# Hybrid attention / RG-LRU / expert kernel on one Trainium2 core: v split by sequence, turned heads on every second step, a postponed first product, and the last expert by column halves

## The chip, the cores and the metric

The kernel runs on one core of one Trainium2 chip. The metric is device time in microseconds (us), lower is better. The engines are PE (TensorE), DVE (VectorE), ACT (ScalarE), POOL (GpSimd) and SP (SyncE, which here only issues DMAs).

## The reference, cut to what matters

One encoder layer, applied with the same weights to two sequences of 512 tokens of width 1024. All data are float32.

```python
h = rmsnorm(x, norm1_g)
q, k, v, xr, gate = split(h @ w_in)          # 8 query heads, 2 key/value heads of 64; LRU width 512
q, k = rope(rmsnorm(q)), rope(rmsnorm(k))
attn_out = softmax(q @ k.T / 8) @ v          # per head, 512 x 512, not causal
lru_out = (scan forward + scan backward of conv(xr)) * gelu(gate)
x = x + concat(attn_out, lru_out) @ w_out
h2 = rmsnorm(x, norm2_g)
# expert choice: each of 16 experts takes its 64 best tokens of each sequence
ys = (silu(xs @ w_gate[e]) * (xs @ w_up[e])) @ w_down[e] * gate_vals
out = x; out[tok_idx] += ys
```

## The kernel before, in words

**Numbers in two parts.** Every matrix product takes a float32 operand as a sum of two rounded parts, `_hi` and `_lo`. ACT writes the hi part, DVE (or POOL) subtracts it from the original for the lo part, and PE makes three matmuls: hi x hi, hi x lo, lo x hi (`product`, lines 972 to 974). Transposes run on PE too, against an identity (line 978), four blocks of 128 x 128 into one PSUM bank.

**Order by hand.** Each engine walks through the same Python list of steps and takes its own part of each; engines meet through semaphores. There is one program order per engine, so whatever stands behind a waiting instruction waits too.

**Stage 1, projections and the LRU.** 28 jobs (7 groups of 4) project the input; `LRU_AT[n]` lists what the engines do beside job n. The last group is the gate of LRU channels; its last job is n = 27. q and k of sequence 0 are rotated, normalised and split here ("rotate", "norm", "hi", "lo"); the last of the ten rotate/norm units (unit 9, k of sequence 1) is left for the attention stage.

**Stage 2, attention.** A list `attn` holds slots 0 to 73. There are 64 units u (16 heads x 4 blocks of 128 queries). In slot u

- PE makes the scores of unit u (two matmuls, lines 1107 and 1108), the four transposes of the probabilities of unit t = u - 6, and the product with v of unit v = u - 8;
- DVE takes the row maximum of unit u (line 1453), the reciprocal of the row sum of unit u - 1 (line 1462), and `probT_lo` of unit t (line 1465);
- ACT writes `probT_hi` of unit t (line 836) and the exponential of unit u (line 843);
- POOL scales the probabilities of unit u - 1 (line 619).

PE's scores of u wait for the exponential of u - 3, its transposes of t for `probT_lo` of t - 3 and, where t begins a head, for all four scaled units of that head; its product of v waits for `probT_lo` of v. Two heads form a pair and add into one bank. Pairs 0, 1 and 2 use the same bank 6, so the first product of pairs 1 and 2 (v = 8 in slot 16, v = 16 in slot 24) waits until ACT and DVE have taken the pair before out of it (`mixA_hi` line 828, `mixA_lo` line 1459), which they do in that same slot.

`beside` (line 374) adds work to single slots. "hi"/"lo" split q and k of blocks 4 to 7 (sequence 1), "v" splits all of v (ACT line 809, then DVE line 1448), "rotate"/"norm" 9 finish unit 9. Twelve "transpose" steps, n = 12 to 23, turn the heads of sequence 1 through the one bank 7 (`turn_heads`): each waits for the "out" step of the one before, in which ACT (even n, line 703) or DVE (odd n, line 1321) copies the bank. Transpose n stands in slot 10 + (n - 12) * 5 // 3 and its out in the slot after. From slot 34 on, the splits of `w_out` and of the LRU output stand there too. SP loads the first three rows of `w_out` once "lo" 7 is done.

**Stage 3** is the output projection, norm and routing. **Stage 4** is a loop over the 16 experts, 24 weight rows each; a row is split by ACT (line 899) and DVE (line 1619) into one of six slots and used by six matmuls (two column halves of 512). At the end ACT scales the expert's output into `ys` (line 914) and POOL adds it to y by an indirect accumulating DMA (`scatter_step`, line 655).

Of the kernel before, what the change touches and what calls it, by code (L numbers as in the profile page):

```python
# [29 lines left out]
P = 128  # L30
# [8 lines left out]
def layer_program(nc, x0, x1, norm1_g, w_in, q_norm_g, k_norm_g, conv_w, conv_b, lru_w_r, lru_b_r,  # L39
# [100 lines left out]
    v_hi = at("v_hi", R1 + 80 * K, [P, NB, VW], F32R)  # L140
    v_lo = at("v_lo", R1 + 90 * K, [P, NB, VW], F32R)
# [19 lines left out]
    assert VW * NB * 4 == 10 * K  # L161
# [30 lines left out]
    gate_all = at("gate_all", SM - 128, [P, E], F32)  # L192

# [150 lines left out]
    lru_at(26, *[(stage, n) for stage in ("transpose", "out") for n in range(BPS)])  # L344
    for n in range(NG * JOBS):
        g, j = ORDER[n]
        if n >= JOBS:
            steps.append(("project", n))
        first = [step for step in LRU_AT.get(n, []) if step[0] in ("scan",)]
        steps += first  # L350
        if n >= JOBS:
            steps.append(("empty", n - 1))
        for w in range(2, NG):
            if n == FIRST_OF[w] - (0, 0, 3, 3, 3, 3, 4)[w]:
                steps += [("w_hi", w), ("w_lo", w)]
        steps += [step for step in LRU_AT.pop(n, []) if step not in first]
# [96 lines left out]
    def v_in(v):  # L453
        return v[:, 1, :, :].rearrange("p b (g w) -> p b g w", g=KVH)
# [4 lines left out]
    def _(sp):  # L459
# [58 lines left out]
        sp.wait_ge(v_lo_done, 1)  # L518
# [66 lines left out]
    def _(pool):  # L585
# [18 lines left out]
        pool.wait_ge(proj_done, NG * JOBS)  # L604
        for v in (v_hi, v_lo):
            pool.memset(v[:, :, :].bitcast(F32).rearrange("p b (g d) -> p b g d", d=HD)[:, :, 0::2, :], 0.0).then_inc(v_zeroed, 1)
# [63 lines left out]
        for e in range(E - 4, E):  # L670
            scatter_step(e, 2 * (E - 4) + e - (E - 4) + 1)

    @block.scalar
    def _(act):
        def prepare(kind, n=0):
# [10 lines left out]
            elif kind == "hi":  # L686
                act.wait_ge(qk_norm_done, units_before(n))
                if n >= BPS:
                    act.wait_ge(rotated, UNITS_QK)
                    act.wait_ge(gates_done, 2 * CT)  # L690
                if n >= BPS + 2:
                    act.wait_ge(qkT_done, last_turn(n - 2) + 1)
                act.activation(q_pair[pair_set(n)][:, :, 0, :].rearrange("p (g h) d -> p g h d", g=2).bitcast(F32R), q_heads(n), ACT.Copy)
                act.activation(k_pair[pair_set(n)][:, :, 0, :, :].bitcast(F32R), k_heads(n).unsqueeze(2).to_broadcast([P, KVH, 2, HD]),
                               ACT.Copy).then_inc(qk_hi_done, 1)

# [10 lines left out]
        for step in steps:  # L707
# [84 lines left out]
            elif kind in PREPARE:  # L792
                prepare(kind, *arg)
            elif kind == "out":
                turn_act(*arg)
# [169 lines left out]
        act.wait_ge(row_used, 24 * E + 8)  # L965
        results(E - 1)

    @block.tensor
    def _(pe):
# [113 lines left out]

        for kind, n in attn:
# [5 lines left out]
            elif kind == "slot":  # L1090
# [24 lines left out]
                if 0 <= v < UNITS:  # L1115
                    head, kc = divmod(v, BPS)
                    pair, s = head // 2, head // HQ
                    if kc == 0 and head % 2 == 0 and pair:
                        pe.wait_ge(mixA_lo_done, pair if pair < PAIRS_ONE_BANK else pair - 1)
                    pe.wait_ge(v_lo_done, 1)  # L1120
                    pe.wait_ge(v_zeroed, 2)
                    pe.wait_ge(probT_lo_done, v + 1)
                    blk, cols = BPS * s + kc, pair_cols(head)
                    product(bank[:, out_bank(pair), :], v_hi[:, blk, cols], v_lo[:, blk, cols], probT_hi[:, kc, :], probT_lo[:, kc, :],
                            head % 2 == 0 and kc == 0, head % 2 == 1 and kc == BPS - 1).then_inc(pv_done, 1)
# [123 lines left out]
        rows(24 * E, 0, 4, hidT_hi, hidT_lo, {})  # L1249

    @block.vector
    def _(dve):
# [15 lines left out]
        def prepare(kind, n=0):  # L1268
# [38 lines left out]
            elif kind == "lo":  # L1307
# [5 lines left out]
                                  kp[:, :, 0, :, :], ALU.subtract).then_inc(qk_lo_done, 1)  # L1313

# [9 lines left out]
        for step in steps:  # L1324
# [104 lines left out]
            elif kind in PREPARE:  # L1429
                prepare(kind, *arg)  # L1430
            elif kind == "out":
# [9 lines left out]
        for kind, n in attn:  # L1441
# [4 lines left out]
            elif kind == "v":  # L1446
                dve.wait_ge(v_hi_done, 1)
                dve.tensor_tensor(v_of(v_lo), v_in(kv_nat), v_of(v_hi).bitcast(F32), ALU.subtract).then_inc(v_lo_done, 1)
# [164 lines left out]
        dve.tensor_copy(gate_all[:, :], bank[:, 6, 0:E]).then_inc(routed, 1)  # L1613

# [91 lines left out]
```

## Time and profile before

| | us |
|---|---|
| three runs | 1057.98, 1058.98, 1059.56 (median 1058.98) |
| the profiled execution | 1058.12 |
| its span, first to last instruction | 1056.2 |
| PE / DVE / ACT / POOL busy | 984.7 / 818.7 / 747.0 / 338.2 |
| mean granted TensorE clock | 0.979 of full speed |

The chain that ended last lies on PE for 82% of the span, on DVE for 7% and on ACT for 5%. By time the kernel has four parts: projections and LRU to about 209 us, attention to about 356, projection and routing to about 477, experts to the end. In a row of the timeline the first number is the start in us from the span's start, the second the duration; in square brackets stands how long the engine had been idle and what ended that.

### The profile page before, as it was taken

To read this page: it belongs to the slowest core of one execution; us is meant where nothing else is said; L and a number is where in the kernel's file an instruction comes from. 1 tells how busy PE (TensorE), PEld (TensorE's weight loads), DVE (VectorE), ACT (ScalarE), POOL (GpSimd) and SP (SyncE) were. 2 spreads that over 40 slices of the span, in tenths; PEclk is the share of its full clock that TensorE was granted. 3 is DMA by queue.
4 is the path that set the end of the run, shared out by engine and by line. 5 is a ranking of instruction groups with operands and counts; after the bars stand their busy time and mean duration, and the time that the engine had idled before them with its cause. 6 is when DMAs were issued, how large, how long until landed. Compare 5 with 4: busy or idle time off the path is not lost.

```text
span 1056.2 us, 15145 instructions
## 1 busy us (share of the span) xinstructions
PE 984.7 (93%) x5035; PEld 826.2 (78%) x5035; DVE 818.7 (78%) x1079; ACT 747.0 (71%) x1002; POOL 338.2 (32%) x175
## 2 busy tenths in 40 slices
PE   5999999977999999928999999999999999999994
PEld 4997998856777788827888888888888888888883
DVE  5749898787787224784989888988898889988983
ACT  6447888467797455545878877887788777877772
POOL 1000000132396111141056435643464346513320
PEclk9999999989999999968999999999999999999998
DMA  8110111000301633368999999999999999999842
GB/s 283 36 46 6 46 40 41 1 0 7 115 1 63 239 120 120 120 242 342 409 392 410 388 384 392 405 386 385 391 400 383 383 393 400 382 384 372 323 163 36
DMA packets 75265, 248.97 MB, mean 236 GB/s; under 512 B 9380, under 2 KB 16600, under 8 KB 75224
## 3 DMA queue, kind: packets, MB, share of 16 engines
q1 hardware_dynamic: 70616, 231.65, 57.1%
q0 software_dynamic: 4608, 16.78, 6.2%
q8 instruction: 25, 0.41, 0.2%
q14 instruction: 16, 0.13, 0.0%
HBM read 231.63 MB, written 16.78 MB: 235 GB/s over the span
## 4 chain that ended last, share of the span: by engine, by line
PE 82%; DVE 7%; ACT 5%; issue 3%; POOL 1%; DMA 1%; ACTq 0%; SPq 0%; POOLq 0%; DVEq 0%
PE bank L972 25%; PE bank L974 24%; PE bank L973 24%; PE bank L978 6%; DVE e_lo L1619 2%; ACT e_hi L899 2%; PE bank L1149 1%; PE bank L1107 1%; PE bank L1108 1%; PE bank L1007 1%; DMA x_nat<-in_x_prompt_dram 1%; ACT prob L843 1%; DMA xs<-h_rows,idx_all 0%; POOL prob L619 0%; DVE row_stat L1453 0%
## 5 line engine op out<-in xcount | busy, mean ns | idle before, releaser
L972 PE MATMUL bank<-e_hi,xsT_hi 128*128 128x512 f32 x512 | 202.4, 395 | 0.7 <-DVE xsT_lo L1624 0.6
L974 PE MATMUL bank<-e_hi,xsT_lo 128*128 128x512 f32 x512 | 200.5, 392 | 0.0
L973 PE MATMUL bank<-e_lo,xsT_hi 128*128 128x512 f32 x512 | 200.1, 391 | 0.0
L651 POOL COPY idx_now<-idx_all 128x1 uint32 (+1 forms) x16 | 157.1, 9818 | 27.2 <-DMA y_dram<-ys,idx_now 27.2
L899 ACT ACTIVATE e_hi<-raw_gate 128x1024 fp32r<-128x1024 f32 x128 | 134.7, 1062 | 35.3 <-PE bank L974 33.7
L1619 DVE TENSOR_TENSOR e_lo<-raw_down,e_hi 128x1024 fp32r<-128x1024 f32 x128 | 146.9, 1219 | 2.4 <-ACT e_hi L899 0.2
L1619 DVE TENSOR_TENSOR e_lo<-raw_gate,e_hi 128x1024 fp32r<-128x1024 f32 x125 | 144.7, 1219 | 4.8 <-ACT e_hi L899 4.7
L1619 DVE TENSOR_TENSOR e_lo<-raw_up,e_hi 128x1024 fp32r<-128x1024 f32 x128 | 146.7, 1219 | 1.4 <-ACT e_hi L899 1.3
L899 ACT ACTIVATE e_hi<-raw_up 128x1024 fp32r<-128x1024 f32 x128 | 126.5, 1057 | 1.3 <-PE bank L974 0.3
L899 ACT ACTIVATE e_hi<-raw_down 128x1024 fp32r<-128x1024 f32 x128 | 125.0, 1058 | 0.4 <-PE bank L974 0.3
L972 PEld LDWEIGHTS bank<-e_hi,xsT_hi 128*128 128x128 f32 x512 | 96.8, 189 | 21.4 <-DVE e_lo L1619 1.0
L974 PEld LDWEIGHTS bank<-e_hi,xsT_lo 128*128 128x128 f32 x512 | 96.7, 189 | 20.6
L973 PEld LDWEIGHTS bank<-e_lo,xsT_hi 128*128 128x128 f32 x512 | 96.9, 189 | 19.8
L972 PE MATMUL bank<-e_hi,hidT_hi 128*128 128x512 f32 x256 | 102.7, 401 | 4.5 <-DVE e_lo L1619 2.9
L973 PE MATMUL bank<-e_lo,hidT_hi 128*128 128x512 f32 x256 | 100.0, 391 | 0.0
L974 PE MATMUL bank<-e_hi,hidT_lo 128*128 128x512 f32 x256 | 99.8, 390 | 0.0
L664 POOL COPY idx_now<-idx_all 128x1 uint32 x12 | 13.6, 1136 | 212.6 <-PE bank L978 212.6
L904 ACT ACTIVATE hidT_hi<-bank 128x512 fp32r<-128x512 f32 x32 | 17.4, 596 | 78.5 <-PE bank L978 78.5
L655 POOL DMA_INDIRECT y_dram<-ys,idx_now x16 | 44.5, 2779 | 78.3 <-ACT ys L914 67.3
L972 PEld LDWEIGHTS bank<-e_hi,hidT_hi 128*128 128x128 f32 x256 | 48.1, 188 | 20.2 <-DVE e_lo L1619 8.5
L619 POOL TENSOR_SCALAR prob<-prob,row_stat 128x512 f32<-128x512 f32 x64 | 45.0, 705 | 57.6 <-DVE row_stat L1462 57.6
L1624 DVE TENSOR_TENSOR hidT_lo<-bank,hidT_hi 128x512 fp32r<-128x512 f32 x32 | 20.6, 686 | 51.2 <-ACT hidT_hi L904 51.2
(241 smaller groups left out, 2193.9 us busy)
## 6 DMA issues: line engine op xcount, KB each, us to landing
raw_gate<-in_exp_w_gate_dram SPq DMA_DIRECT2D x64, 1024.0 KB, 10.8
raw_up<-in_exp_w_up_dram SPq DMA_DIRECT2D x64, 1024.0 KB, 8.2
raw_down<-in_exp_w_down_dram SPq DMA_DIRECT2D x64, 1024.0 KB, 7.0
w_raw<-in_w_in_dram SPq DMA_DIRECT2D x6, 1024.0 KB, 5.4
wo_raw<-in_w_out_dram SPq DMA_DIRECT2D x8, 512.0 KB, 4.2
y_dram<-x SPq DMA_DIRECT2D x8, 512.0 KB, 5.1
h_rows<-h SPq DMA_DIRECT2D x8, 512.0 KB, 2.6
x_nat<-in_x_prompt_dram SPq DMA_DIRECT2D x4, 512.0 KB, 7.5
```

The source lines that it names most:

```text
L619: pool.tensor_scalar(prob[:, u % PROB_SLOTS, :], prob[:, u % PROB_SLOTS, :], row_stat[:, 2, u:u + 1], 1.0, ALU.mult, ALU.mult).then_inc(pr ...
L651: pool.tensor_copy(idx_now[:, 2:3], idx_all[:, bass.ds(e, 1)] if not isinstance(e, int) else idx_all[:, e:e + 1]).then_inc(idx_copied, 1)
L655: pool.indirect_dma_start(y, bass.IndirectOffsetOnAxis(ap=idx_now[:, 2:3], axis=0), ys[:, :], None, compute_op=ALU.add).then_inc(scattered ...
L664: pool.tensor_copy(idx_now[:, parity:parity + 1], idx_all[:, bass.ds(e + (parity + 4), 1)]).then_inc(idx_copied, 1)
L899: act.activation(e_hi[:, (8 * m + j) % SPLIT, :], raw[:, j // 2, j % 2, :], ACT.Copy).then_inc(row_hi, inc)
L904: act.activation(out[:, 4 * h:4 * h + 4, :], bank[:, 6 + h, :].rearrange("p (k t) -> p k t", k=4), ACT.Copy).then_inc(out_done, 1)
L972: pe.matmul(out, l_hi, r_hi, start=first, stop=False)
L973: pe.matmul(out, l_hi, r_lo, start=False, stop=False)
L974: return pe.matmul(out, l_lo, r_hi, start=False, stop=last)
L978: ins = pe.transpose(bank[:, out_bank, i * P:(i + 1) * P], piece, ident[:, :])
L1619: dve.tensor_tensor(e_lo[:, slot, :], raw[:, j // 2, j % 2, :], e_hi[:, slot, :].bitcast(F32), ALU.subtract).then_inc(row_lo, inc)
L1624: dve.tensor_tensor(out[:, 4 * h:4 * h + 4, :], bank[:, 6 + h, :].rearrange("p (k t) -> p k t", k=4), hi[:, 4 * h:4 * h + 4, :].bitcast(F3 ...
```

## The change

- v is held in two tiles for each part, one per sequence (`v_hi[0]`, `v_hi[1]`, `v_lo[0]`, `v_lo[1]`), placed so that those of sequence 0 need only projection jobs 0 to 23. "v" 0, "rotate" 9 and "norm" 9 move to job 27 of stage 1; "v" 1 moves to slot 16. POOL's two zero fills become four of half the size, the first two after job 23.
- "hi"/"lo" of blocks 4 to 7 stand two to three slots earlier.
- Transpose n of sequence 1 stands in slot 6 + 2 * (n - 12), and every "out" from n = 8 on in the same slot as its transpose.
- The first product of pairs 1 and 2 is made one slot later, ahead of the next one.
- The last expert's down rows 2 to 7 are used first for column half 0 and then for half 1; each half is scaled and added to y by a DMA of its own, for which DVE makes an index 2 * i + h.

```diff
+    v_hi = [at(f"v_hi{s}", R1 + o * K, [P, BPS, VW], F32R) for s, o in enumerate((80, 90))]
+    v_lo = [at(f"v_lo{s}", R1 + o * K, [P, BPS, VW], F32R) for s, o in enumerate((97, 85))]
...
+    lru_at(27, ("v", 0), ("rotate", UNITS_QK - 1), ("norm", UNITS_QK - 1))
...
-    beside = {2: [('v', 0)], 3: [('rotate', 9)], 4: [('norm', 9)], 6: [('hi', 4)], 7: [('lo', 4)], 10: [('hi', 5)], 11: [('lo', 5)], 15: [('hi', 6)], 16: [('lo', 6)], 22: [('hi', 7)], 23: [('lo', 7)]}
+    beside = {3: [("hi", 4)], 4: [("lo", 4)], 8: [("hi", 5)], 9: [("lo", 5)], 13: [("hi", 6)], 14: [("lo", 6)],
+              16: [("v", 1)], 19: [("hi", 7)], 20: [("lo", 7)]}
     for n in range(2 * BPS, USES * NB):
-        at_slot = n - 2 * BPS + 1 if n < EARLY else 10 + (n - EARLY) * 5 // 3
+        at_slot = n - 2 * BPS + 1 if n < EARLY else 6 + (n - EARLY) * 2
         beside.setdefault(at_slot, []).append(("transpose", n))
-        beside.setdefault(at_slot + 1, []).append(("out", n))
+        beside.setdefault(at_slot, []).append(("out", n))
...
+    def late_pair(v):
+
+        return v % (2 * BPS) == 0 and 0 < v // (2 * BPS) < PAIRS_ONE_BANK
+
+    def pv_at(u):
+
+        v = u - V_LAG
+        if not 0 <= v < UNITS or late_pair(v):
+            return []
+        return [v - 1, v] if late_pair(v - 1) else [v]
...
         sp.wait_ge(qk_lo_done, NB)
-        sp.wait_ge(v_lo_done, 1)
+        sp.wait_ge(v_lo_done, SEQS)
...
+        for s in range(SEQS):
+            pool.wait_ge(proj_done, NG * JOBS if s else (NG - 1) * JOBS)
+            for v in (v_hi[s], v_lo[s]):
+                pool.memset(v[:, :, :].bitcast(F32).rearrange("p b (g d) -> p b g d", d=HD)[:, :, 0::2, :], 0.0).then_inc(v_zeroed, 1)
...
+        pool.wait_ge(routed, 3)
+        for h in range(2):
+            pool.wait_ge(ys_done, E + 1 + h)
+            pool.sem_inc(scatter_ready, 1)
+            pool.indirect_dma_start(y_halves, bass.IndirectOffsetOnAxis(ap=idx_half[:, h:h + 1], axis=0),
+                                    ys[:, h * D // 2:(h + 1) * D // 2], None, compute_op=ALU.add).then_inc(scattered, 16)
...
-        act.wait_ge(row_used, 24 * E + 8)
-        results(E - 1)
+        act.wait_ge(ys_free, E)
+        for h in range(2):
+            act.wait_ge(row_used, 24 * E + 8 - SPLIT + h + 1)
+            act.activation(ys[:, h * D // 2:(h + 1) * D // 2], bank[:, 4 + h, :], ACT.Copy, scale=gate_all[:, E - 1:E]).then_inc(ys_done, 1)
...
+        for h in range(2):
+            for j in range(8 - SPLIT, 8):
+                if h == 0:
+                    pe.wait_ge(row_lo, 24 * E + j + 1)
+                ins = last_product(j, h)
+            ins.then_inc(row_used, 1)
```

## Rows read from the trace of the kernel before

**Rows 1.** Windows: busy time of each engine in the first attention stretch; columns named.

```profile
core 0: us, PE busy (x) PEld busy (x) DVE busy (x) ACT busy (x) POOL busy (x), PEclk, DMA share, GB/s
...
209.00:270.00 61.00, 47.52 (x255) 37.50 (x254) 46.54 (x97) 40.94 (x95) 19.61 (x27) 0.92 0.07 27
```

**Rows 2.** Waits of PE in attention (207 to 356): us in total, times, longest.

```profile
PE bank L978 <- POOL prob L619: 6.7, 4, 3.3
PE bank L972 <- DVE mixA_lo L1459: 3.3, 2, 1.9
PE bank L978 <- DVE kT L1321: 2.9, 2, 1.5
...
PE bank L978 <- ACT kT L703: 2.5, 2, 1.2
```

**Rows 3.** Timeline of PE, slots 6 to 8 of attention.

```profile
216.92 0.51 PE L1107 MATMUL bank<-kT,qT 128*128 128x512 f32 x1 [2.61 <-ACT prob L843]
...
221.00 1.12 PE L978 MATMUL bank<-ident,prob 128*128 128x128 f32 x4 [3.35 <-POOL prob L619]
...
225.19 0.78 PE L972 MATMUL bank<-probT_hi,v_hi 128*128 128x512 f32 x1
```

**Rows 4.** Timelines of DVE and POOL about the start of attention.

```profile
208.05 0.69 DVE L1385 TENSOR_TENSOR lru_out<-lru_out,bank 128x512 f32<-128x512 f32 x1 [4.70 <-ACT bank L744]
...
214.23 1.22 DVE L1448 TENSOR_TENSOR v_lo<-kv_nat,v_hi 128x1024 fp32r<-128x1024 f32 x1 [1.71 <-ACT v_hi L809]
...
216.05 0.67 DVE L1294 TENSOR_TENSOR turned<-kv_nat,tab 128x512 f32<-128x512 f32 x1
...
218.45 0.68 DVE L1321 CAST qT<-bank 128x512 fp32r<-128x512 f32 x1
...
207.39 1.38 POOL L606 MEMSET v_hi<- 128x1536 f32 x1 [178.63 <-PE bank L974]
```

**Rows 5.** Timeline of PE: scores of slots 12 and 29, products 8 and 16.

```profile
233.53 0.47 PE L1107 MATMUL bank<-kT,qT 128*128 128x512 f32 x1
...
243.35 0.50 PE L972 MATMUL bank<-probT_hi,v_hi 128*128 128x512 f32 x1 [1.41 <-DVE mixA_lo L1459]
...
263.56 0.50 PE L972 MATMUL bank<-probT_hi,v_hi 128*128 128x512 f32 x1 [1.90 <-DVE mixA_lo L1459]
...
275.16 0.48 PE L1107 MATMUL bank<-kT,qT 128*128 128x512 f32 x1
```

**Rows 6.** One slot's pitch on DVE and PE (timelines); ACT and DVE groups (lines).

```profile
295.50 0.67 DVE L1465 TENSOR_TENSOR probT_lo<-bank,probT_hi 128x512 fp32r<-128x512 f32 x1
...
296.75 0.67 DVE L1465 TENSOR_TENSOR probT_lo<-bank,probT_hi 128x512 fp32r<-128x512 f32 x1
...
305.68 0.40 PE L1107 MATMUL bank<-kT,qT 128*128 128x512 f32 x1
...
307.28 0.40 PE L1107 MATMUL bank<-kT,qT 128*128 128x512 f32 x1
...
L843 ACT ACTIVATE prob<-bank,row_stat 128x512 f32<-128x512 f32 x29 | 20.0, 691 | 6.8 <-DVE row_stat L1453 6.6
...
L1310 DVE TENSOR_TENSOR q_pair<-q_nat,q_pair 128x512 fp32r<-128x512 f32 x4 | 2.9, 720 | 0.0
```

**Rows 7.** Windows of 1 us with the clock at its lower level (columns as Rows 1).

```profile
220.00:221.00 1.00, 0.00 (x0) 0.00 (x0) 1.00 (x4) 1.00 (x3) 0.95 (x1) 0.50 0.00 0
264.00:265.00 1.00, 1.00 (x4) 0.81 (x3) 0.16 (x1) 0.21 (x1) 0.36 (x1) 0.50 0.98 377
```

**Rows 8.** Timeline of the last expert's down rows and result; last, its DMA.

```profile
1033.94 0.50 PE L972 MATMUL bank<-e_hi,hidT_hi 128*128 128x512 f32 x1 [1.57 <-DVE hidT_lo L1624]
1034.03 6.90 DVE L1619 TENSOR_TENSOR e_lo<-raw_down,e_hi 128x1024 fp32r<-128x1024 f32 x6
...
1045.20 1.12 ACT L914 ACTIVATE ys<-bank,gate_all 128x1024 f32<-128x1024 f32 x1 [6.46 <-PE bank L974]
1047.10 1.57 POOL L655 DMA_INDIRECT y_dram<-ys,idx_now  x1 [13.72 <-ACT ys L914]
...
y_dram<-ys,idx_now POOLq DMA_INDIRECT x1, 6.1
```

More of the change, by code:

```diff
@@ L695, in prepare, with split_v_hi @@
                                ACT.Copy).then_inc(qk_hi_done, 1)
+        def split_v_hi(s):
+            act.wait_ge(proj_done, NG * JOBS if s else (NG - 1) * JOBS)
+            act.wait_ge(kv_out, JOBS)
+            act.activation(v_of(v_hi[s]), v_in(s), ACT.Copy).then_inc(v_hi_done, 1)
         def turn_act(n):
@@ L807, in _ @@
             elif kind == "v":
-                act.wait_ge(proj_done, NG * JOBS)
-                act.activation(v_of(v_hi), v_in(kv_nat), ACT.Copy).then_inc(v_hi_done, 1)
+                split_v_hi(n)
             elif kind == "out":
@@ L1082, in project_out, with weigh_values @@
             return ins
+        def weigh_values(v):
+            head, kc = divmod(v, BPS)
+            pair, s = head // 2, head // HQ
+            if kc == 0 and head % 2 == 0 and pair:
+                pe.wait_ge(mixA_lo_done, pair if pair < PAIRS_ONE_BANK else pair - 1)
+            pe.wait_ge(v_lo_done, s + 1)
+            pe.wait_ge(v_zeroed, 2 * (s + 1))
+            pe.wait_ge(probT_lo_done, v + 1)
+            cols = pair_cols(head)
+            product(bank[:, out_bank(pair), :], v_hi[s][:, kc, cols], v_lo[s][:, kc, cols], probT_hi[:, kc, :], probT_lo[:, kc, :],
+                    head % 2 == 0 and kc == 0, head % 2 == 1 and kc == BPS - 1).then_inc(pv_done, 1)
         for kind, n in attn:
@@ L1114, in _ @@
                     transposes(SCORE_BANKS + t % TURN_BANKS, [prob[:, (BPS * head + qb) % PROB_SLOTS, kc * P:(kc + 1) * P] for qb in range(BPS)], probT_done)
[L1115 to L1125, printed above, removed]
+                for v in pv_at(u):
+                    weigh_values(v)
         def turn_x2(b):
@@ L1248, in _, with last_product @@
         pe.wait_ge(ys_done, E)
-        rows(24 * E, 0, 4, hidT_hi, hidT_lo, {})
+        def last_product(j, h):
+            cols = slice(h * 512, (h + 1) * 512)
+            return product(bank[:, 4 + h, :], hidT_hi[:, j, :], hidT_lo[:, j, :], e_hi[:, j % SPLIT, cols], e_lo[:, j % SPLIT, cols],
+                           j == 0, j == 7)
+        for j in range(8 - SPLIT):
+            pe.wait_ge(row_lo, 24 * E + j + 1)
+            for h in range(2):
+                ins = last_product(j, h)
+            ins.then_inc(row_used, 1)
+        for h in range(2):
+            for j in range(8 - SPLIT, 8):
+                if h == 0:
+                    pe.wait_ge(row_lo, 24 * E + j + 1)
+                ins = last_product(j, h)
+            ins.then_inc(row_used, 1)
     @block.vector
@@ L1446, in _ @@
             elif kind == "v":
[L1447 to L1448 removed]
+                split_v_lo(n)
             elif kind == "slot":
@@ L1613, in _ @@
         dve.tensor_copy(gate_all[:, :], bank[:, 6, 0:E]).then_inc(routed, 1)
+        dve.wait_ge(routed, 1)
+        for h in range(2):
+            ins = dve.tensor_scalar(half_row[:, h:h + 1], idx_all[:, E - 1:E], 2.0, float(h), ALU.mult, ALU.add)
+        link(ins)
+        dve.tensor_copy(idx_half[:, :], half_row).then_inc(routed, 1)
         def lo_row(first, m, raw, j, inc=1):
```

24 lines of the change are left out of this document (15 added, 9 removed).

## The prediction

> **What bounds the kernel now.** I read the engine shares first: PE is busy nearly everywhere, so the places to look for are those where it is not. The windows by stage name one that the change touches: in the 61 us from 209 to 270, PE is busy 47.5 us and its mean granted clock is 0.92, and no other engine is full either (DVE 46.5) [rows 1]. So engines wait for each other there. PE's waits over all of attention name for whom: the scaled probabilities (6.7 us, four times), the emptying of bank 6 (3.3, twice), and the copy of turned k heads out of bank 7, by DVE (2.9, twice) and by ACT (2.5, twice) [rows 2]. The timeline then gives their times: of the 6.7 us one wait of 3.35 stands at slot 6, right behind one of 2.61 for an exponential [rows 3]; the other three lie beyond slot 30, where nothing is changed. After this stretch the kernel is a chain on PE whose starts are all released by attention's end, so time won there should be kept.
>
> **The start of attention (slots 0 to 8).** DVE had v_lo in slot 2 (1.22 us, after waiting 1.71 for v_hi) and rotate 9 in slot 3 (216.05 to 218.45, 2.40 us), norm 9 in slot 4 (about 0.6); every row maximum behind them is late, then the exponentials, POOL's scaling, and PE [rows 3, 4]. The change moves half of v, the rotation and the norm to job 27. There DVE was idle for 4.70 us until the last gate multiplication at 208.05 [rows 4]; the moved work is 0.6 + 2.4 + 0.6 = 3.6 us, so about 1 us of cover is left, and the gate multiplication, behind which the last head turn of slot 0 waits, should not be late. POOL's fills (1.38 us each before) are halved, two of them lie under the projections, and the others end before POOL has anything to scale: nothing. Walking the slots with the durations of the rows: DVE's maximum of unit 3 comes at 213.0; ACT then has hi 4 (about 1.0) and a copy ahead of exponential 4, DVE has lo 4 (about 0.95) and a copy ahead of maximum 5 at 217.0; PE turns the first probabilities at 215.6 instead of 221.00 and waits about 0.9 us at the first turn of sequence 1, since its bank copy of slot 4 ends near 217.1. The first product starts at 219.8 instead of 225.19: 5.4 us won. Of these, 2.6 are the clock alone: PE's work from 221.0 to 226.3 ran at the lower level (1.2 GHz) after the two waits [rows 7], and in the new order PE is never idle for more than about 1 us there. The scores of slot 12 come at 226.0 instead of 233.53, **7.5 us won**; the extra 2 us are one bank-7 wait (1.24) and what was left of the slow clock.
>
> **Slots 12 to 29.** Here PE needed 275.16 - 233.53 = 41.6 us [rows 5]. In it are three bank-7 waits (the 5.4 us of [rows 2] less the first of 1.24: 4.1), the two bank-6 waits of 1.41 and 1.90 [rows 5], and 1.5 us of lower clock behind the second [rows 7]; without all of these 32.7 are left. A turn on every second slot leaves a whole slot for the copy, so the bank-7 waits go. What is late next is **DVE together with ACT**. A slot costs PE 1.60 us, about 1.95 with a turn; it costs DVE 1.25 [rows 6], but maximum, exponential (0.69) and the next probT_hi follow one another between the two engines, and this loop gives some 1.36 a slot once both lag (my estimate from these durations). To that DVE has 0.6 for each of 4 copies in slots 5 to 16, 0.95 for each of lo 5 and lo 6 [rows 6], and in slot 16 mixA_lo, v_lo 1 and another copy, 1.8 us in all. Because PE now starts 7.5 us earlier and never waits for long, DVE doesn't catch up: its maximum of slot 16 comes at about 236.6. So **the postponed product does not find its bank empty**: PE reaches product 8, in slot 17, at 236.2, mixA_lo ends near 238.0, and a wait of 1.8 us remains; at product 16 one of 1.2. Without the postponement each would be some 1.2 to 1.6 longer. Slot 19 comes at 241.5 (249.77 before), slot 26 at 255.3 and slot 29 at 261.2, instead of 275.16: **14.0 us won up to there**, 6.5 of them in this part (35.2 us instead of 41.6: the 32.7, the two bank-6 waits of 3.0 less a turn that now comes earlier).
>
> **What else is queued.** SP's first loads of w_out come with lo 7, in slot 20 instead of 23; the added wait for v 1 (slot 16) is older. They are needed from slot 34: nothing. Slots 34 to 62 keep their steps and their waits on POOL; I take them as unchanged (bounds: 1.5 better, 3.3 worse, the size of these waits). The index work adds four tiny DVE instructions after routing, under the gather of the first tokens: nothing, 0.5 us if uncovered.
>
> **The last expert.** Rows 2 to 7 are ready at DVE's pace, six in 6.90 us from 1034.03, so row 7 at 1040.93; half 0 uses a row in 3 matmuls, 0.68 us. PE, at row 2 by 1036.84, runs into rows 6 and 7, waits about 0.3 and 0.45 us, ends half 0 at 1041.7 and half 1 4.1 us later, with restarts at about 1045.9, 0.7 later than before [rows 8]. Then the scaling of a half is some 0.6 us (ACT's other copies of 128 x 512 take 0.6 to 0.7) instead of 1.12; POOL's issue still takes 1.57, and the DMA has half the bytes. It took 6.1 us from issue to landing [rows 8]; no row shows one of half the size. Bounds: 6.1 (as long, if its 128 rows set the time) and 4.1 (if the bytes set the 4 us in which it moved). I take 5.1, the middle. Sum: +0.7 - 0.5 - 1.0 = **0.8 us won** (from 0.2 lost to 1.8 won).
>
> The Trainium skill has a price for this: "DMA: Bandwidth & Descriptors", section "Anatomy of one DMA — SWDGE (gpsimd) path", puts a DMA from GpSimd at about 2.0 us plus its bytes at 436 GB/s. By it, half the bytes save an estimated 0.6 us, not 1.0, and the tail would win 0.4; for the whole it gives 3.2 us where the row has 6.1, so the trace does not agree on the size.
>
> **Sum.** 14.0 + 0.8 = 14.8 us; I take off 0.3 for latencies that the walk leaves out. The profiled execution took 1058.12 (1.92 more than its span), which gives 1043.6; the median of the runs is 0.86 above that execution, hence **1044.5**.
>
> **Rivals.** *A, the forecast* (DVE and ACT bound slots 9 to 26): 1044.5, of itself 1042.5 to 1047; chance 0.56. *B, PE bound*: DVE and ACT keep up, all waits go; then slots 12 to 29 cost 17 x 1.60 + 9 turns at 0.42 = 31.0 us from 226.0, slot 29 comes at 257.0, 4.2 us earlier, 1040.3. For it: DVE has slack in the slots after 275. Against: 46.5 busy us of 61 and the work is the same. 0.10. *C, the clock falls all the same*: PE keeps waits of 0.9, 1.8 and 1.2 us, and the second low stretch came behind a wait of only 1.90 [rows 5, 7]. If both low stretches stay, 2.6 + 1.5 come back: 1048.6. 0.22. The Trainium skill has a rule that speaks for it ("TensorE: Matmul & The Clock Gate", section "A second HAM failure mode: psum-queue depth-cycling"): short idle times between groups of matmuls, as PE cycles through PSUM banks, make the clock swing between its levels. The trace agrees in part: behind 1.90 us it fell, behind 1.41 at 243.35 it did not. *D, given back later*: the lag of DVE and ACT (some 4 us) is carried into slots 34 to 62, where POOL's waits double: 3.3 back, 1047.8. 0.06. *E, the early steps don't do what they say*: ACT or DVE reaches the last gate multiplication late and the head of attention slips by what v, rotate and norm cost there, 3.6 us: 1048.1. 0.03. *F, slower*: denser but shorter waits hold the clock at its lower level through attention. At that level each us loses half, so the gain of 14.8 is gone when it lasts 29 us, and beyond 34 us the kernel is over 0.2% slower; held through all of slots 6 to 34 (50 us) it gives 1069. Against: the longest low stretch in this stage was about 6 us. 0.03.
>
> **How the numbers follow.** 0.2% (2.1 us) is about what a measurement can tell from no change. Only F, and a small part of C, is not faster: faster 0.95, same 0.02, slower 0.03. The range takes A's own range, C, D, E and half of B: 1041.0 to 1050.0.
>
> **What would show it.** In the new trace: no low clock before slot 12; first product near 219.8; DVE without idle time of 1 us from 215 to 235; no PE wait for kT or qT copies above 0.6; still a wait of 1 to 2 us for mixA_lo before products 8 and 16; slot 29 near 261; the interval from slot 34 to routing unchanged within 1 us; in the last product two waits below 0.5 us for split rows and an end 0.7 us later after its first matmul than before; the last DMA landing about 5 us after its issue. The prediction is wrong if the last gate multiplication is later than 208.1, if the mixA_lo waits are gone (then B), or if the low clock returns (C).

## The result, and the profile after

The changed kernel takes **1043.63 us** (median of 4 runs, 1041.57 to 1044.46), the kernel before in the same session 1058.59 (1057.98 to 1059.56): a ratio of **0.9855, with a 95% interval of 0.9838 to 0.9872**. Measured again in a later session (five runs) it gave 1042.88 against 1060.25, 0.9839 [0.9825, 0.9852]. The forecast was 1044.5 with a range of 1041.0 to 1050.0.

The profiled execution took 1041.57 us, its span is 1039.5. The stretch of [rows 1], by windows (PE, PEld, DVE, ACT and POOL busy; then the granted clock), and PE's waits in attention, as in [rows 2]:

```profile
209.00:270.00 61.00, 57.01 (x336) 46.23 (x335) 54.01 (x120) 49.97 (x122) 23.54 (x34) 1.00 0.14 53
```

```profile
PE bank L1011 <- POOL prob L635: 3.6, 4, 1.5
PE bank L1005 <- DVE mixA_lo L1519: 2.3, 2, 1.5
...
PE bank L1011 <- DVE qT L1380: 0.9, 1, 0.9
```

PE is busy 57.0 of the 61 us (47.5 before), the clock is full throughout (0.92 before), DVE is up from 46.5 to 54.0. (The same 61 us now reach further into the list of slots, 336 matmuls instead of 255, so the two rows are not the same work; slots are compared below.) The waits for kT copies (5.4 us) are gone; of the waits for POOL the one of 3.35 is gone, the three beyond slot 30 are as they were; the waits for mixA_lo went from 3.3 to 2.3 us and did not vanish.

The timeline of PE, with the lines that answer to [rows 3, 5]: scores of slot 6, first turn of probabilities, first turn of sequence 1, first product, scores of slot 12, products 8 and 16, scores of slot 29.

```profile
213.47 0.50 PE L1153 MATMUL bank<-kT,qT 128*128 128x512 f32 x1 [0.27 <-ACT prob L874]
214.45 0.66 PE L1011 MATMUL bank<-ident,prob 128*128 128x128 f32 x4 [0.25 <-POOL prob L635]
216.05 0.63 PE L1011 MATMUL bank<-ident,k_pair 128*128 128x128 f32 x4 [0.94 <-DVE qT L1380]
218.67 0.47 PE L1005 MATMUL bank<-probT_hi,v_hi 128*128 128x512 f32 x1
225.10 0.39 PE L1153 MATMUL bank<-kT,qT 128*128 128x512 f32 x1
236.57 0.50 PE L1005 MATMUL bank<-probT_hi,v_hi 128*128 128x512 f32 x1 [1.51 <-DVE mixA_lo L1519]
252.28 0.50 PE L1005 MATMUL bank<-probT_hi,v_hi 128*128 128x512 f32 x1 [0.78 <-DVE mixA_lo L1519]
259.37 0.47 PE L1153 MATMUL bank<-kT,qT 128*128 128x512 f32 x1
```

One correction comes first. In this execution slot 0 starts at 208.17, in the profiled one of before at 209.27. That 1.10 is not the change's (last section), so I count from the start of slot 0:

| us from the start of slot 0 | before | after | won |
|---|---|---|---|
| slot 0 to first product | 15.92 | 10.50 | 5.42 |
| slot 0 to slot 12 | 24.26 | 16.93 | 7.33 |
| slot 12 to slot 29 | 41.63 | 34.27 | 7.36 |
| **slot 0 to slot 29** | **65.89** | **51.20** | **14.69** |
| slot 29 to slot 63 | 57.77 | 57.75 | 0.02 |
| first matmul of the last product to the end | 22.26 | 21.56 | 0.70 |

From the scores of slot 63 to the last product the two differ by 0.19 us (701.01 and 700.82). With the 1.10 at slot 0 this accounts for all of the 16.7 us between the two spans.

The same stretch, slots 0 to 29, as windows (columns as above), first before, then after:

```profile
209.27:275.16 65.89, 51.26 (x280) 40.69 (x279) 49.55 (x104) 43.45 (x102) 20.59 (x29) 0.92 0.07 25
208.17:259.37 51.20, 47.21 (x281) 38.05 (x279) 44.81 (x100) 42.09 (x102) 19.06 (x28) 1.00 0.09 32
```

The work of PE is the same in both. Its idle time (length less busy time) went from 14.63 to 3.99 us, and its busy time for the same work fell by 4.05 us, which is what the lower clock cost before.

DVE's last gate multiplication, the first line of [rows 4], and then the last product and the result, as in [rows 8] (timelines, and the DMA's issues with the us to landing):

```profile
206.95 0.69 DVE L1444 TENSOR_TENSOR lru_out<-lru_out,bank 128x512 f32<-128x512 f32 x1 [1.32 <-ACT bank L774]
```

```profile
1017.94 0.50 PE L1005 MATMUL bank<-e_hi,hidT_hi 128*128 128x512 f32 x1 [1.57 <-DVE hidT_lo L1689]
...
1024.99 0.50 PE L1005 MATMUL bank<-e_hi,hidT_hi 128*128 128x512 f32 x1 [0.18 <-DVE e_lo L1684]
...
1026.05 0.69 ACT L999 ACTIVATE ys<-bank,gate_all 128x512 f32<-128x512 f32 x1 [3.32 <-PE bank L1007]
1030.08 0.69 ACT L999 ACTIVATE ys<-bank,gate_all 128x512 f32<-128x512 f32 x1 [3.34 <-PE bank L1007]
...
1031.56 1.54 POOL L693 DMA_INDIRECT y_dram<-ys,idx_half  x1 [2.50 <-ACT ys L999]
...
y_dram<-ys,idx_half POOLq DMA_INDIRECT x2, 4.7
```

DVE's idle time ahead of the last gate multiplication shrank from 4.70 to 1.32 us, and the multiplication stands 1.22 us before slot 0 in both kernels: not late. In the tail the last scaling starts 12.14 us after the product's first matmul (11.26 before), POOL issues 1.48 behind it (1.90 before), and the end is 7.94 behind the issue (9.10 before).

### The profile page after: what moved, and what is told of

Read it like the earlier page. It is cut to its first block, busy times and chain, and to the rows that moved or that the text cites. A ratio compares the mean times of both kernels' runs of the same rounds, so it can differ in the third digit from the quotient of the medians.

```text
span 1039.5 us, 15156 instructions
## 1 busy us (share of the span) xinstructions
PE 979.6 (94%) x5035; PEld 822.2 (79%) x5035; DVE 817.3 (79%) x1083; ACT 745.9 (72%) x1004; POOL 340.3 (33%) x177
## 4 chain that ended last, share of the span: by engine, by line
PE 83%; DVE 7%; ACT 4%; issue 2%; DMA 1%; POOL 1%; ACTq 0%; DVEq 0%; SPq 0%; POOLq 0%
PE bank L1005 25%; PE bank L1007 24%; PE bank L1006 24%; PE bank L1011 6%; DVE e_lo L1684 2%; ACT e_hi L930 2%; PE bank L1187 1%; PE bank L1154 1%; PE bank L1153 1%; PE bank L1040 1%; DMA x_nat<-in_x_prompt_dram 1%; DMA xs<-h_rows,idx_all 0%; DVE row_stat L1513 0%; DVE xc L1453 0%; DVE work L1594 0%
## 5 line engine op out<-in xcount | busy, mean ns | idle before, releaser
L671 POOL DMA_INDIRECT y_dram<-ys,idx_now x15 | 44.1, 2939 | 64.5 <-ACT ys L945 53.5
```

The source lines that it names most:

```text
L671: pool.indirect_dma_start(y, bass.IndirectOffsetOnAxis(ap=idx_now[:, 2:3], axis=0), ys[:, :], None, compute_op=ALU.add).then_inc(scattered ...
```

## The experiments

My theory: DVE and ACT, not PE, set the pace from slot 9 to 26; the early steps remove work from their queues at the worst place, the spread turns give each copy a slot's time, and what is still late is the emptying of bank 6. Six experiments start from the changed kernel and undo or alter one thing; three have the tail undone and only one of the other three parts left in; two alter several things at once. **All of them keep v in two halves (v 1 in slot 16, or later), splits hi and lo that are moved against the kernel before, the copies of sequence 0's turned heads in the slot of their turn, and the small index work on DVE.** So the three single ones are not the kernel before plus one edit. The expectations of two of them name a part of this rest only, and that of the last says "nothing else of the change", which its edit does not bear out; this matters below. For each I give the time and the intervals from the start of slot 0.

**The early steps undone.** v 0 goes back to slot 2 and rotate 9 to slot 3; norm 9 goes to slot 3 too (it was in slot 4 before).

```diff
-    lru_at(27, ("v", 0), ("rotate", UNITS_QK - 1), ("norm", UNITS_QK - 1))
...
-    beside = {3: [("hi", 4)], 4: [("lo", 4)], 8: [("hi", 5)], 9: [("lo", 5)], 13: [("hi", 6)], 14: [("lo", 6)],
+    beside = {2: [("v", 0)], 3: [("rotate", 9), ("norm", 9), ("hi", 4)], 4: [("lo", 4)], 8: [("hi", 5)], 9: [("lo", 5)], 13: [("hi", 6)], 14: [("lo", 6)],
```

> The changed kernel with v of sequence 0, rotate 9 and norm 9 put back into slots 2 and 3 of attention (everything else as changed). Theory, DVE and ACT lag behind PE from slot 5 on: the 3.6 us of DVE work return ahead of the first row maxima, the first product comes 3.6 to 5.5 us later, and slot 29 as much later, since DVE has no idle time in which to make it good; if PE's waits are long enough for the granted clock to fall to 0.50 before slot 8, another 2 to 2.6 us. Median 1047.5 to 1051. Rival, PE bound after slot 12: the later slots make part of it good, because PE's waits for mixA_lo (1.51 and 0.78 us) shrink; at most 2.5 us slower, 1046.

1047.91 us, ratio to before 0.9896 [0.9879, 0.9913]. As the theory had it (1047.5 to 1051, rival 1046). The first product comes 17.10 us after slot 0 instead of 10.50, slots 0 to 12 take 23.56 us instead of 16.93, slots 12 to 29 only 32.95 instead of 34.27. The two large waits of [rows 3] are back:

```profile
216.78 0.50 PE L1152 MATMUL bank<-kT,qT 128*128 128x512 f32 x1 [2.49 <-ACT prob L873]
220.65 1.11 PE L1010 MATMUL bank<-ident,prob 128*128 128x128 f32 x4 [3.13 <-POOL prob L634]
```

The turn of the probabilities (second line) lasts 1.11 us instead of 0.66: the low clock is back with them. And PE, 6.6 us later, then waits only 0.51 at product 8 (1.51 in the changed kernel): DVE and ACT do lag behind an earlier PE, and 1.3 us of what the early steps win is paid back to that.

**The turns undone.** Heads of sequence 1 turned in three slots out of five, two of them neighbours, and copied a slot after the turn, as before.

```diff
-        at_slot = n - 2 * BPS + 1 if n < EARLY else 6 + (n - EARLY) * 2
+        at_slot = n - 2 * BPS + 1 if n < EARLY else 10 + (n - EARLY) * 5 // 3
...
-        beside.setdefault(at_slot, []).append(("out", n))
+        beside.setdefault(at_slot + (n >= EARLY), []).append(("out", n))
```

> The changed kernel with the turned heads of sequence 1 at their old slots (10 + (n - 12) * 5 // 3) and their copies one slot after. Theory of the lag: four waits of PE for the copy out of bank 7 come back (1.2 to 1.5 us each, 5.4 in all), but DVE and ACT catch up during them, so the two waits for mixA_lo (2.3 us in all) go: 3 us slower, 1046.7. Rival, each part is worth the waits that it removes: 5.4 us slower, 1049. Third: the copies are as late as the slots anyway, under 1 us.

1053.91 us, 0.9951 [0.9934, 0.9969]; slots 0 to 29 take 63.96 us, **12.8 more** than in the changed kernel, beyond what any of the theories gave (3, 5.4, under 1). PE's waits at the second turn of each pair, and one window with its clock:

```profile
228.86 0.63 PE L1011 MATMUL bank<-ident,q_pair 128*128 128x128 f32 x4 [2.62 <-ACT kT L733]
...
242.96 0.63 PE L1011 MATMUL bank<-ident,q_pair 128*128 128x128 f32 x4 [3.70 <-DVE kT L1380]
...
256.73 0.63 PE L1011 MATMUL bank<-ident,q_pair 128*128 128x128 f32 x4 [2.01 <-ACT kT L733]
...
269.52 0.63 PE L1011 MATMUL bank<-ident,q_pair 128*128 128x128 f32 x4 [1.41 <-DVE kT L1380]
```

```profile
230.00:234.00 4.00, 4.00 (x16) 3.32 (x15) 2.80 (x6) 1.74 (x4) 1.16 (x2) 0.57 0.01 2
```

The four waits are 9.74 us. In [rows 2] the turns cost 5.4, but 3.3 for mixA_lo came on top, 8.7 in all; here no wait for mixA_lo is left. Of the 12.8 us, 7.6 are idle time of PE and 5.2 are longer busy time: PE's work at the lower clock behind three of the waits. (The profiled execution was the slowest of its four, 1.1 us above their median. By the run times the turns are worth about 11 us: 1053.91 against the 1043.50 of the kernel with only the tail undone, in the same session, and 0.78 for the tail.) A second turn right behind the first can't start until the first one's copy is out of bank 7, and that copy stands in the lagging queue of ACT or DVE: PE pays the **whole** lag there, and the clock falls to 0.57 behind it. These waits do not grow because the rest of the kernel is better: with the early steps undone as well (the last of the single parts below) they are 9.6 us.

**The first products not put off.**

```diff
-        return v % (2 * BPS) == 0 and 0 < v // (2 * BPS) < PAIRS_ONE_BANK
+        return False
```

> The changed kernel with the first product of pairs 1 and 2 in its old slot (16 and 24). Theory of the lag: mixA_lo comes when DVE comes to it, whatever PE does, so PE only waits earlier and longer (some 3 and 2 us instead of 1.51 and 0.78) and slots 18 and 26 begin 1.1 us later each at most, part of which is made good: 1 to 2 us slower, 1044.6 to 1045.6; if the longer wait lets the clock fall to 0.50, 1.5 more. Rival: the postponement is what removed the waits of before, 1.41 and 1.90: 3.3 us slower, 1047. Third: nothing, 1043.6.

1045.8 us, 0.9878 [0.986, 0.9895]; slots 0 to 29 take 53.24 us, 2.04 more. That is the theory of the lag (waits of some 3 and 2 us), 0.2 us beyond its range, and not the rival's 1047. The waits for mixA_lo are 3.11 and 1.64 us instead of 1.51 and 0.78:

```profile
237.44 0.50 PE L1005 MATMUL bank<-probT_hi,v_hi 128*128 128x512 f32 x1 [3.11 <-DVE mixA_lo L1519]
```

```profile
238.00:242.00 4.00, 4.00 (x26) 3.32 (x25) 3.37 (x8) 2.25 (x6) 1.08 (x3) 1.00 0.00 0
```

Behind the wait of 3.11 the clock stays at 1.00, unlike behind the 2.62 above.

**The tail undone**: the last expert's product, scaling and DMA as in the kernel before.

```diff
-        for h in range(2):
-            act.wait_ge(row_used, 24 * E + 8 - SPLIT + h + 1)
-            act.activation(ys[:, h * D // 2:(h + 1) * D // 2], bank[:, 4 + h, :], ACT.Copy, scale=gate_all[:, E - 1:E]).then_inc(ys_done, 1)
+        act.wait_ge(row_used, 24 * E + 8)
+        results(E - 1)
```

> The changed kernel with the last expert as before (all rows with both column halves, one scaling, one DMA). From its traces, the last product's first matmul to the end of the span took 22.26 us before and 21.56 after: that interval goes back to 22.3, the last matmul starts 10.83 us after the first instead of 11.71, and POOL's last issue to the end takes 9.1 us instead of 7.9. 0.7 us slower in all, 1044.3, which a time can hardly tell. Rival: the difference is the end of the execution that varies by itself; then the interval stays 21.6.

1043.5 us (1042.04 to 1045.91), 0.9853 [0.9828, 0.9879]: by the time of the runs it can't be told from the changed kernel. The interval from the last product's first matmul to the end can: 22.36 us here, and 22.26, 22.21 and 22.29 in the three other profiles with the old tail and a full clock there; 21.56, 21.39, 21.70, 21.44 and 21.41 in five with the new one. Means 22.28 and 21.50: **0.78 us**. The rival, an end that varies by itself, is out: the two groups do not overlap.

**Only one of the parts.** The early steps alone, the turns alone, the postponement alone, each on the common rest named above.

> Of the change only: v by sequence, rotate 9 and norm 9 in job 27, hi/lo of blocks 4 to 7 earlier; turned heads, products and the last expert as before. The scores of slot 0 to those of slot 29 take 65.9 us before and 51.2 changed. Theory (PE pays the whole lag of DVE and ACT at each back-to-back pair of turned heads, as the waits of 2.62, 3.70, 2.01 and 1.41 us in the kernel with the old turns suggest): 64 to 66 us, the earlier start is lost again at the first of these waits; median 0 to 2.5 us below before. Rival, the early steps are worth what their undoing cost (5.3 us): 60.6 us.

1057.26 us, 0.9981 [0.997, 0.9993]; slots 0 to 29: 64.19 us, as the theory had it (64 to 66; rival 60.6). PE waits 2.63, 1.41, 2.02 and 1.40 us for bank 7, and twice for mixA_lo:

```profile
239.89 0.50 PE L995 MATMUL bank<-probT_hi,v_hi 128*128 128x512 f32 x1 [1.34 <-DVE mixA_lo L1493]
...
263.05 0.50 PE L995 MATMUL bank<-probT_hi,v_hi 128*128 128x512 f32 x1 [0.94 <-DVE mixA_lo L1493]
```

All six are 9.74 us. This kernel has the old turns and the products in their old slots; with the products put off (the turns undone, above) four waits are left, and they are 9.74 us as well. The same sum is collected at six places here and at four there.

> Of the change only: turned heads of sequence 1 at every second slot with the copy in the same slot, and the hi/lo steps that they need earlier; v 0, rotate 9 and norm 9 stay in slots 2 and 3, products and the last expert as before. Theory: no wait for bank 7, so slots 0 to 29 take 58 to 59 us (7 to 8 us won; 56.5 with the products put off, 2.0 more without). Rival, additive with the undoing of the turns (12.8 us): 53 us. Third, the waits that it removes (5.4 us) and no more: 60.5.

1051.04 us, 0.9921 [0.9899, 0.9944]; slots 0 to 29: 59.97 us. The theory (58 to 59) is missed by 1 us, the third case (60.5) by 0.5. No wait for bank 7 above 0.45 is left; those for mixA_lo are 1.84 and 1.61 us.

> The kernel before with the first product of two head pairs put off by one slot, and nothing else of the change. In the kernel before the waits for the mix at products 8 and 16 are 1.41 and 1.90 us, the second followed by a stretch at half clock. Theory 1 (a term of its own, as the prediction has it, 1.2 to 1.6 each): the two waits go, slots 0 to 29 take 61.0 to 63.2 us instead of 65.89. Theory 2 (the lag of VectorE and ScalarE is paid elsewhere): with the turned heads still back to back, TensorE waits as much longer at the next copies, and slots 0 to 29 take 64.5 to 66 us.

1061.77 us, 1.0009 [0.9999, 1.0019]; slots 0 to 29: **68.94 us**, 3.05 more than in the one profile of the kernel before and outside both theories (61.0 to 63.2, 64.5 to 66). The waits for mixA_lo are gone, and three of those for bank 7 are 8.2 us alone:

```profile
232.73 0.63 PE L1000 MATMUL bank<-ident,q_pair 128*128 128x128 f32 x4 [2.32 <-ACT kT L724]
...
245.65 1.09 PE L1000 MATMUL bank<-ident,q_pair 128*128 128x128 f32 x4 [3.88 <-DVE kT L1353]
...
260.51 0.63 PE L1000 MATMUL bank<-ident,q_pair 128*128 128x128 f32 x4 [2.01 <-ACT kT L724]
```

Put together, slots 0 to 29 in us:

| early steps | turns spread | put off | us | of these PE idle | mean clock |
|---|---|---|---|---|---|
| yes | yes | yes | 51.20 | 3.99 | 1.00 |
| no | yes | yes | 56.51 | 7.39 | 0.94 |
| yes | yes | no | 53.24 | 6.35 | 1.00 |
| no | yes | no | 59.97 | 9.51 | 0.91 |
| yes | no | yes | 63.96 | 11.55 | 0.92 |
| yes | no | no | 64.19 | 11.48 | 0.92 |
| no | no | yes | 68.94 | 15.42 | 0.88 |
| kernel before | | | 65.89 | 14.63 | 0.92 |

Read in pairs: spreading the turns is worth 11.0 to 12.8 us (5.1 to 8.0 of idle time, 4.4 to 5.8 of lower clock), the early steps 5.0 to 6.7 (3.2 to 3.9 idle, the rest clock), the postponement 2.0 and 3.5 with spread turns (2.4 and 2.1 idle) and **0.2** with the old ones, where the lag is paid at bank 7 instead. Each row is one execution, and the share of the clock can differ from one to the next (last section); the idle times are the firmer column.

The parts sum to more than 14.7. With the old turns the combination "no, no, no" would be near 69.2 (an estimate: 68.94 and the 0.23 of the pair 64.19 and 63.96), 3.3 us above the kernel before. That this is a price of the common rest is not shown. The row of the last single part against the profile of the kernel before:

```profile
208.38:277.32 68.94, 53.52 (x281) 42.36 (x279) 49.88 (x105) 43.36 (x103) 19.44 (x28) 0.88 0.06 24
```

Only 0.8 of its 3.05 us are idle time, 2.3 are lower clock; and by the run times this kernel is between 0.1 us faster and 2.0 us slower than the one before (1.0009 [0.9999, 1.0019]). If the rest has a price, it is nearer 1 us than 3. What differs is chiefly that hi and lo stand two or three slots earlier, right ahead of the old pairs of turns in slots 10 and 11, 15 and 16, and that v 1 is in slot 16, within the second pair. No run took one of these alone.

**What makes the wait at product 8.** All turned heads of sequence 1 copied by ACT, none by DVE:

```diff
-            if n % 2 == 0:
+            if n % 2 == 0 or n >= EARLY:
...
-            if n % 2:
+            if n % 2 and n < EARLY:
```

> The changed kernel with all twelve copies of turned heads of sequence 1 on ACT (before: six on ACT, six on DVE). Theory, DVE's own work is what lags: 0.6 us less in slots 8, 12, 16, 20, 24, 28; the waits for mixA_lo (1.51 and 0.78 us) go and slots 0 to 29 take 49 us instead of 51.2; median 1041.5. Rival, the loop of maximum, exponential and probT_hi over both engines sets the pace: ACT's copies delay the next probT_hi by as much as DVE wins, 51 to 52 us, 1043.6 or slower.

1042.6 us, 0.9845 [0.9827, 0.9863]; slots 0 to 29 take 50.27. The wait at product 16 is gone, the one at product 8 is 1.51 as before: the result lies between the two theories. DVE's timeline in the changed kernel shows why the copies don't matter at product 8 (it stood idle for 0.83 us, for ACT, before what is listed; what its earlier copies cost was used up there):

```profile
232.26 0.69 DVE L1525 TENSOR_TENSOR probT_lo<-bank,probT_hi 128x512 fp32r<-128x512 f32 x1 [0.83 <-ACT probT_hi L867]
232.87 0.68 DVE L1364 TENSOR_TENSOR q_pair<-q_nat,q_pair 128x512 fp32r<-128x512 f32 x1
233.47 0.42 DVE L1366 TENSOR_TENSOR k_pair<-kv_nat,k_pair 128x256 fp32r<-128x256 f32 x1
233.81 0.68 DVE L1513 TENSOR_REDUCE row_stat<-bank 128x1 f32<-128x512 f32 x1
...
235.82 0.69 DVE L1519 TENSOR_TENSOR mixA_lo<-bank,mixA_hi 128x512 fp32r<-128x512 f32 x1
```

What stands ahead of mixA_lo is lo 6 (L1364, L1366: 0.94 us), then the maximum of unit 15, its exponential, and mixA_hi on ACT.

So lo 6 was moved behind it. The edit does more than its expectation says: hi 6 and lo 6 go two slots later (13 and 14 to 15 and 16), v 1 goes from slot 16 to 26, and the tail is split as in the next paragraph. v 1 stood behind mixA_lo in slot 16, so it cannot be what moves mixA_lo:

```diff
-    beside = {3: [("hi", 4)], 4: [("lo", 4)], 8: [("hi", 5)], 9: [("lo", 5)], 13: [("hi", 6)], 14: [("lo", 6)],
-              16: [("v", 1)], 19: [("hi", 7)], 20: [("lo", 7)]}
+    beside = {3: [("hi", 4)], 4: [("lo", 4)], 8: [("hi", 5)], 9: [("lo", 5)], 15: [("hi", 6)], 16: [("lo", 6)],
+              26: [("v", 1)], 19: [("hi", 7)], 20: [("lo", 7)]}
```

> The changed kernel with the upper and the lower part of head 6's v block turned one slot later each (slots 15 and 16), v 1 of the next load at 26, and the last product in halves of four and four rows blocks. In the changed kernel VectorE does lo 6 (0.94 us) at 232.87, straight ahead of max 15 (233.81), max 16 (235.06) and the eviction of the mix of product 8 (235.82), for which TensorE stands 1.51 us. Theory (VectorE's order makes this wait): the mix comes about 0.9 earlier, the wait at product 8 falls from 1.51 to about 0.6, slots 0 to 29 take 50.3 us instead of 51.20, and with the tail's 0.9 to 1.1 the kernel is about 1.8 us faster than the changed one. Rival (the work is only moved): lo 6 is then late for product 9 or for what TensorE wants in slot 18, a wait of 0.5 to 1.0 stands there, slots 0 to 29 take 51.0 to 51.4 and only the tail's 1 us is won.

1042.28 us, 0.9837 [0.9824, 0.9851]; slots 0 to 29 take 50.60, the wait is 1.11 instead of 1.51 (0.6 expected). For the slots that is two thirds of what the theory gave, and the timeline names the rest: DVE now stands idle for ACT. The whole kernel was to be 1.8 us faster than the changed one; beside it in the same session (1042.88) it is 0.6 us faster by the medians, with overlapping intervals.

```profile
234.25 0.65 ACT L717 ACTIVATE q_pair<-q_nat 128x512 fp32r<-128x512 f32 x1
234.77 0.43 ACT L718 ACTIVATE k_pair<-kv_nat 128x256 fp32r<-128x256 f32 x1
235.07 0.61 ACT L859 ACTIVATE mixA_hi<-bank 128x512 fp32r<-128x512 f32 x1
...
235.72 0.69 DVE L1519 TENSOR_TENSOR mixA_lo<-bank,mixA_hi 128x512 fp32r<-128x512 f32 x1 [0.69 <-ACT mixA_hi L859]
```

hi 6, moved along with lo 6, now stands ahead of mixA_hi on ACT. Measured from slot 0, mixA_lo starts at 27.01 us instead of 27.65: 0.64 earlier, not 0.9. The price moved from one engine's queue to the other's.

**The tail split evenly**: in the last product only rows 4 to 7 by column halves, instead of rows 2 to 7 (SPLIT is 6).

```diff
-        for j in range(8 - SPLIT):
+        for j in range(4):
...
-            for j in range(8 - SPLIT, 8):
+            for j in range(4, 8):
```

> The changed kernel with the last expert's column halves made apart only for rows 4 to 7, not 2 to 7. DVE has each split row ready before PE comes to it, so the last matmul starts 10.85 us after the first instead of 11.71; the first half is still issued over 1.5 us ahead of the second. First matmul of the last product to the end: 20.7 us instead of 21.56. Rival: the two DMAs now follow each other closely (2.7 us apart instead of 4.0) and the second lands later by as much: 21.5.

1043.03 us, 0.9849 [0.9832, 0.9867]; from the first matmul to the end 20.64 us, 0.9 less than with the change's split.

```profile
1027.22 0.69 ACT L999 ACTIVATE ys<-bank,gate_all 128x512 f32<-128x512 f32 x1 [3.77 <-PE bank L1007]
1029.88 0.69 ACT L999 ACTIVATE ys<-bank,gate_all 128x512 f32<-128x512 f32 x1 [1.97 <-PE bank L1007]
```

The product starts at 1018.66 here, so the last scaling comes 11.22 us after it instead of 12.14: PE waits for no row any more. That gap of 0.9 was a loss inside the changed kernel's own tail. The rival (the second DMA lands later, now that the two are issued 2.7 us apart) is out: from its issue to the end it takes 7.94 us in both. The run times do not tell this kernel from the changed one.

**Together** (lo 6 later, copies on ACT, tail split evenly), beside the changed kernel itself:

> As e7_lo6_later, and all copies of turned heads of sequence 1 on ScalarE (as in e5_copies_on_act, which alone took slots 0 to 29 from 51.20 to 50.27 by removing the wait at product 16 and left 1.51 at product 8). Theory (the two are separate terms): both waits for the mix are small, slots 0 to 29 take about 49.3 us, the kernel is about 2.7 us faster than the changed one. Rival (ScalarE, busy 20.7 of 24 us already in e5, is the bound): TensorE waits for exponentials or copies instead and slots 0 to 29 take 50.3 us or more.

> The changed kernel itself, beside the two others on one chip, so that they can be compared with it and not only with the kernel before. Expected 1043.6 us and 51.2 us for slots 0 to 29; the start of slot 0 between 208.1 and 209.6 us, as it was from execution to execution in the other runs.

1041.02 us (1040.65 to 1042.7), 0.9824 [0.981, 0.9837], against 1042.88 (1041.05 to 1044.46) for the changed kernel in the same session. Slots 0 to 29 take 49.89 and 51.17 us; the wait at product 8 is 1.11, that at product 16 gone. It wins 1.28 us there where 1.9 was expected, and ACT is not a wall. By the medians it is 1.9 us faster than the changed kernel (2.7 expected), but the two intervals overlap; what the profiles show without doubt are the 1.3 us in attention.

## Why the prediction came out

**Start of attention.** Right by its own steps. Cover left at the last gate multiplication: about 1 us forecast, 1.32 measured. Wait at the first turn of sequence 1: 0.9 and 0.94. First product 5.4 us earlier and 5.42; slot 12 7.5 earlier and 7.33. No wait above 0.94, no low clock before slot 12. (One of the signs named, no wait for a qT copy above 0.6, contradicts the forecast's own 0.9 at that turn; it holds from slot 12 on only.)

**Slots 12 to 29.** Right in kind, and too cautious by 0.9 us: 6.5 us forecast, 7.36 measured. "Set the pace" says too much of DVE and ACT, though: PE is busy for 31.9 of the 34.27 us, and their lag shows at two places only. DVE has no idle time of 1 us between 215 and 235 (the largest gap is 0.83), no wait for a kT or qT copy above 0.6 is left there, and the waits for mixA_lo stay, 1.51 and 0.78 us instead of 1.8 and 1.2. The terms that were mis-sized are these two, since the walk put mixA_lo 0.3 to 0.4 us too late at each. It gives DVE four copies in slots 5 to 16 besides that of slot 16; DVE made two there, in slots 8 and 12, and ACT three. That points the same way, but no run shows that it is the cause. The postponement was priced at 1.2 to 1.6 a product; undone, the two waits grew by 1.60 and 0.86, and slots 0 to 29 by 2.04.

The one step of the argument that the runs correct does not show in the total: the sum took away "three bank-7 waits, 4.1 us" and "two bank-6 waits" as separate amounts. They are one lag, that of DVE and ACT, paid wherever PE next needs them. With old turns in the otherwise changed kernel no wait for bank 6 is left, and those for bank 7 are 9.74 us, not 5.4: they take over what bank 6 had. With the products in their old slots as well, both kinds together are 9.74 us again. The total held because the walk was made for the new order as a whole and not by subtraction. The clock's share was right: 2.6 and 1.5 us forecast, 4.05 us less busy time measured.

**What else is queued.** Slots 29 to 63 take 57.75 us instead of 57.77, as forecast; the waits for POOL there keep their lengths. Rival D falls with that.

**The tail.** 0.8 forecast, 0.70 in the profiles compared and 0.78 over nine of them. By terms: last scaling 0.88 later (0.7 forecast), scaling and POOL 0.42 sooner (0.5), the DMA: 1.16 less from issue to the end (1.0 forecast; landing 6.1 and 4.7 us). The price of the Trainium skill ("DMA: Bandwidth & Descriptors", section "Anatomy of one DMA — SWDGE (gpsimd) path") gave a saving of 0.6 for half the bytes; the row gives 1.4 in landing time, so the trace does not agree, on the slope as little as on the whole.

**Rival C.** The clock did not fall: 1.00 in all windows from 209 to 270. PE kept waits of 0.94, 1.51 and 0.78 us, as forecast, and none brought it down; the rule of the Trainium skill on short idle times that the prediction weighed ("TensorE: Matmul & The Clock Gate", section "A second HAM failure mode: psum-queue depth-cycling") was not at work in this kernel. That holds in the second profile of it as well, and in six of kernels that differ from it in the tail, the copies, lo 6 or the postponement: all eight read 1.00 in slots 0 to 29. Rival B was as wrong as thought: the waits for mixA_lo are there, and its 31.0 us for slots 12 to 29 was too low in any case, since PE's own work in them takes 31.6 to 31.9 us. Rival E fell with the gate multiplication in its place.

**The sum.** 14.69 and 0.7 make 15.4, against 14.5 forecast; the medians differ by 14.96. The step from one profiled execution to the median of the runs was put at 0.86 us and measured 2.06 (1041.57 to 1043.63). So part of the closeness to 1044.5 is luck: 0.9 us more were won and slot 0 happened to start 1.1 us earlier in the profile, and 1.2 us of this step stand against that.

## What to carry to other kernels

Where two engines lag together behind PE, their lag is one debt, and each wait in the profile is only the place where PE happens to collect it: don't add up the waits that an edit removes, walk the new order through and ask where the engine is needed next. Two uses of one buffer in neighbouring steps are the dearest such place, since PE pays all of the lag there. And a step moved off one engine's path drags its partner on the other engine along: look at both queues.

## What the runs showed of the hardware

**The clock falls or rises at different moments where the work is the same.** The end of the first projections is the same code in all these kernels; one matmul of the same shape at the same moment of the kernel before and of the changed one:

```profile
20.34 0.41 PE L973 MATMUL bank<-hT_lo,w_hi 128*128 128x256 f32 x1
```

```profile
20.40 0.28 PE L1005 MATMUL bank<-hT_hi,w_hi 128*128 128x256 f32 x1
```

Matmuls get short from 21.41 us on in the kernel before and from 19.06 in the changed one, PE being busy without a gap from 15.8 us on in both; the next stage starts at 22.20 and 21.12. These are the 1.1 us by which the two traces differ at slot 0. Over the fourteen profiles matmuls get short between about 18.7 and 22 us and slot 0 starts between 208.01 and 209.57, while from the start of the next stage to slot 0 it is 187.04 to 187.10 us in all fourteen. (The column of the granted clock reads 1.00 on both sides of the step, so that it is the clock is inferred: matmuls of one shape start 0.21 us apart ahead of it and 0.12 behind it, under the same work.)

The last product has the same two gaps in all kernels. First line: the kernel with lo 6 later; second: the one with the copies on ACT as well, with a window of it.

```profile
1019.11 0.50 PE L1005 MATMUL bank<-e_hi,hidT_hi 128*128 128x512 f32 x1 [1.57 <-DVE hidT_lo L1689]
```

```profile
1016.78 0.80 PE L1007 MATMUL bank<-e_hi,hidT_hi 128*128 128x512 f32 x1 [1.57 <-DVE hidT_lo L1691]
...
1018.00:1019.00 1.00, 1.00 (x3) 0.79 (x3) 1.00 (x2) 1.00 (x2) 0.00 (x0) 0.50 0.00 0
```

In the first the clock stays full, in the second it is at 0.50 for some 3 us, and the tail takes 22.12 us instead of 20.59. So it was in three of the fourteen profiles, with the old tail (23.65 us instead of 22.3) and with the new one (22.09 instead of 21.5). With a wait of 3.11 us that left the clock at 1.00 and one of 2.62 that brought it to 0.57, the length of a wait alone does not say whether the clock falls. What decides it, no run here shows. It moves one execution by 1 to 1.5 us at each such place, which is as much as the smaller parts of this change are worth: they had to be read from intervals inside the trace, not from the whole time. Inside attention the same holds for the part of an interval that is lower clock.
